# Differential attention: the combination of the two maps, shared by VectorE and GpSimd in single tiles of keys from five tiles on

## The reference

```python
def block(args):
    qi, st = args
    sc = jnp.einsum('bhmqd,bhmkd->bhmqk', qi, k).astype(jnp.float32) * scale
    mask = kpos[None, :] <= (st + jnp.arange(Q_BLOCK))[:, None]
    p = jax.nn.softmax(jnp.where(mask, sc, -jnp.inf), axis=-1)
    a = p[:, :, 0] - lam * p[:, :, 1]
    return jnp.einsum('bhqk,bhkd->bhqd', a.astype(v.dtype), v)
```

## Time and profile before

| | us |
|---|---|
| median of 3 runs | 2376.82 |
| the profiled execution | 2375.63 |
| its span, first to last instruction | 2373.8 |
| PE busy | 2285.4 |
| DVE busy | 1749.2 |
| ACT busy | 975.2 |
| POOL busy | 354.6 |

### The profile page before, as it was taken

The page is one execution under the profiler, slowest core; times in us unless marked ns, Lnnn a source line. Parts: engine busy times, 40 slices in busy tenths (PEclk is TensorE's granted clock), DMA queues, the critical chain, the costliest instruction groups (busy, mean ns, idle before and its releaser), DMA issues.

```text
span 2373.8 us, 31336 instructions
## 1 busy us (share of the span) xinstructions
PE 2285.4 (96%) x11618; PEld 1926.3 (81%) x11618; DVE 1749.2 (74%) x2660; ACT 975.2 (41%) x1598; POOL 354.6 (15%) x281
## 2 busy tenths in 40 slices
PE   5999999987999999999999999999999999999999
PEld 3987897766889888888888888888888888888887
DVE  5558796978989876877676767677687676767676
ACT  4532555458888854432322222233432322223231
POOL 0343043823355630000000000000000000000000
PEclk8999999988999999999999999999999999999999
DMA  7441434120000052111111111135101111111112
GB/s 261 156 155 46 151 116 151 49 98 27 15 14 23 10 163 77 54 54 36 62 44 55 51 53 53 53 123 195 63 28 44 62 44 53 53 53 53 53 53 88
DMA packets 108280, 177.68 MB, mean 75 GB/s; under 512 B 5512, under 2 KB 77468, under 8 KB 107164
## 3 DMA queue, kind: packets, MB, share of 16 engines
q1 hardware_dynamic: 108188, 176.45, 22.5%
HBM read 152.84 MB, written 23.59 MB: 74 GB/s over the span
## 4 chain that ended last, share of the span: by engine, by line
PE 83%; DVE 8%; DMA 3%; ACT 2%; issue 2%; POOL 1%; SPq 1%; ACTq 0%; DVEq 0%
PE ps L2486 10%; PE ps L2484 10%; PE ps L2485 10%; PE ps L2522 7%; PE ps L2521 7%; PE ps L2523 7%; PE ps L2187 6%; PE ps L2188 6%; PE ps L2189 6%; PE ps L2374 2%; PE ps L2431 2%; PE ps L2429 2%; PE ps L2430 2%; PE ps L2359 2%; DVE sb_scores L1816 2%
## 5 line engine op out<-in xcount | busy, mean ns | idle before, releaser
L1974 DVE TENSOR_TENSOR sb_x_new<-sb_x_new,ps 128x512 f32<-128x512 f32 x512 | 347.2, 684 | 107.6 <-PE ps L2486 102.0
L2484 PE MATMUL ps<-sb_w_hi,sb_u_hi 128*128 128x512 f32 x1024 | 398.3, 389 | 0.0
L2485 PE MATMUL ps<-sb_w_lo,sb_u_hi 128*128 128x512 f32 x1024 | 398.3, 389 | 0.0
L2486 PE MATMUL ps<-sb_w_hi,sb_u_lo 128*128 128x512 f32 x1024 | 398.3, 389 | 0.0
L2486 PEld LDWEIGHTS ps<-sb_w_hi,sb_u_lo 128*128 128x128 f32 x1024 | 192.3, 188 | 39.9
L2484 PEld LDWEIGHTS ps<-sb_w_hi,sb_u_hi 128*128 128x128 f32 x1024 | 192.3, 188 | 39.9
L2485 PEld LDWEIGHTS ps<-sb_w_lo,sb_u_hi 128*128 128x128 f32 x1024 | 192.3, 188 | 39.8
L2189 PE MATMUL ps<-sb_h_hi,sb_w_lo 128*128 128x512 f32 x512 | 199.4, 389 | 0.0
L1418 ACT ACTIVATE ps<-ps 128x512 f32<-128x512 f32 x28 | 16.3, 582 | 410.8 <-PE ps L2523 410.8
L2187 PE MATMUL ps<-sb_h_hi,sb_w_hi 128*128 128x512 f32 x448 | 178.0, 397 | 0.7 <-DVE sb_w_lo L1935 0.7
L2188 PE MATMUL ps<-sb_h_lo,sb_w_hi 128*128 128x512 f32 x448 | 174.4, 389 | 0.0
(11 more groups left out here) (286 smaller groups left out, 4955.4 us busy)
## 6 DMA issues: line engine op xcount, KB each, us to landing
sb_w_full<-in_w_ff SPq DMA_DIRECT2D x34, 1024.0 KB, 5.1
sb_w_full<-in_w_ff SPq DMA_DIRECT2D x56, 512.0 KB, 3.8
sb_w_raw<-in_w_in SPq DMA_DIRECT2D x16, 1024.0 KB, 5.7
sb_ada<-in_w_ada SPq DMA_DIRECT2D x32, 512.0 KB, 5.3
sb_ada_first<-in_w_ada SPq DMA_DIRECT2D x8, 1024.0 KB, 14.3
sb_x_in<-in_x SPq DMA_DIRECT2D x16, 512.0 KB, 4.9
sb_mix_in<-mix_scratch SPq DMA_DIRECT2D x16, 512.0 KB, 5.1
sb_x_new<-in_x SPq DMA_DIRECT2D x16, 512.0 KB, 4.8
```

What stands on the lines that cost most here:

```text
L1974: V.tensor_tensor(out=y, in0=y, in1=psum[:, 4 + p % 4, :], op=ALU.add).then_inc(ff2_read, 1)
L2484: M(dst, uh, wh[:, j, col], start=j == order[0], stop=False, skip_group_check=fast)
L2485: M(dst, uh, wl[:, j, col], start=False, stop=False, skip_group_check=fast)
L2486: ins = M(dst, ul, wh[:, j, col], start=False, stop=j == order[1], skip_group_check=fast)
```

## The change

The split is now made in tiles and not in groups: from n = 5 on, DVE has the first half of the tiles, rounded up, and POOL the rest. DVE's part at n = 5 to 16 goes from 5, 6, 7, 4, 8, 8, 8, 8, 8, 8, 8, 8 tiles to 3, 3, 4, 4, 5, 5, 6, 6, 7, 7, 8, 8. POOL's goes from 0, 0, 0, 4, 1, 2, 3, 4, 5, 6, 7, 8 to 2, 3, 3, 4, 4, 5, 5, 6, 6, 7, 7, 8. PE waits for POOL at the group that holds POOL's first tile, which is group 0 at n = 5 and 6, group 1 at n = 7 to 14, and group 2 at n = 15 and 16. The counters of `upper_ready` now count the units with a POOL part from unit 16 on. n = 8, 15 and 16 keep their sizes.

```diff
 def upper(u):
-    n = len(at_groups(u))
-    return (n + 1) // 2 if u // HEADS + 1 >= 8 else n
+    n = u // HEADS + 1
+    return (n + 1) // 2 if n >= 5 else n
...
-UPPER_NO = running(int(upper(u) < len(at_groups(u))) for u in range(UNITS))
+UPPER_NO = running(int(upper(u) < u // HEADS + 1) for u in range(UNITS))
...
             def combine_upper(u):
-                n, c0 = (u // HEADS + 1) * P, upper(u) * BLK
+                n, c0 = (u // HEADS + 1) * P, upper(u) * P
                 if c0 < n:
                     pool.wait_ge(a_ready, u + 1)
...
-                both = upper(u) * BLK < n
+                both = upper(u) * P < n
                 if both and UPPER_NO[u] >= 4:
                     dve.wait_ge(upper_ready, UPPER_NO[u] - 3)
-                n = min(n, upper(u) * BLK)
+                n = upper(u) * P
...
                     if f == 0:
                         pe.wait_ge(a_ready, i + 1)
-                    if f == upper(i):
-                        pe.wait_ge(upper_ready, UPPER_NO[i] + 1)
+                    if f == upper(i) // 4 and UPPER_NO[i + 1] > UPPER_NO[i]:
+                        pe.wait_ge(upper_ready, UPPER_NO[i + 1])
```

## The result

The changed kernel takes 2392.43 us (median of five runs, 2391.16 to 2394.78), the kernel before 2379.27 in its five (2375.77 to 2383.40): the ratio is 1.0058, interval 1.0043 to 1.0072. It is slower, as forecast and inside the range, but by 13.2 us between the medians. The forecast's sum was +9.2 on one execution of 2375.63; the profiled execution of the changed kernel took 2394.78, which is +19.2. So the direction was right, and the sum was about half of what the two traces show.

What follows compares the result with a forecast made beforehand. In the attention at n = 5 to 14, PE, DVE and ACT, all nearly full, wait for each other. Terms -4.5 + 8.8 + 2.5 + 2.4 = +9.2 us on 2375.63 give 2384.8, as median 2386.0; range 2373 to 2393.

Steps and rivals of the forecast that it cites:

- term 4: PE's clock: one fall to half speed after the wait at n = 6, +2.4 us, bounds 0 and +8.
- a difference as a sign of being wrong: Behind the attention no slack was seen; a difference showing there would mean the forecast is wrong.
- part 2: POOL's long block of root and scalings delays PE at n = 6, 10 and 14: +4.0, +3.0, +1.8, sum +8.8 us.
- parts 1 and 3: Shorter DVE combinations at n = 5 to 14, -4.5 us; DVE held by POOL's instructions, +2.5 us.
- more falls of the clock: Rival: the clock falls at n = 10 and 14 too, +5 us on top, 2391; chance 0.13.
- Absorbed: Rival: PE makes up the block's delays and holds fall where DVE waits anyway, +0.4 us, 2377.2; chance 0.17.
- faster: Rival: three quarters of the shorter combinations' gain returns, the block costs only plain extra time, -5.5 us, 2371.3; chance 0.15.
- PE waits in every unit of n = 5 and 6: Rival: PE waits for POOL at group 0, +2.4 us to the forecast, 2388.4; chance within the forecast's 0.55.

Runs made afterwards that it cites:

- e4: Changed kernel with PE's waits for POOL at units 22, 38 and 54 filled by 50, 36 and 40 identity transposes: 2387.58 us, ratio 1.0028.
- e3: Changed kernel with the split by tiles at n = 5 to 8 only, by groups of four from n = 9 as before: 2388.68 us, ratio 1.0030.
- e12: Changed kernel with POOL's inverse root and scalings mostly left out, for timing only: 2368.44 us, ratio 0.9949.
- e13: Kernel before with POOL's inverse root and scalings mostly left out, for timing only: 2372.41 us, ratio 0.9963.
- e1: Changed kernel with POOL's block cut in three, the first scaling one step later and the second two steps later: 2392.15 us, ratio 1.0044.
- e9: Changed kernel with POOL's block in five pieces, PE's turns moved, and squares, sums and root one step later still: 2368.28 us, ratio 0.9946.
- e11: Changed kernel split by tiles from n = 8 only, block in five pieces, turns moved, squares, sums and root a step later: 2373.70 us, ratio 0.9964.
- e10: Kernel before with POOL's block in five pieces, PE's turns moved, squares, sums and root one step later: 2372.68 us, ratio 0.9962.
- e6: Changed kernel with POOL's block cut in five pieces and PE's turns of finished rows moved later: 2374.29 us, ratio 0.9969.
- e8: Changed kernel split by tiles from n = 8 only, with POOL's block in five pieces and PE's turns moved: 2375.92 us, ratio 0.9971.
- e7: Kernel before with POOL's block cut in five pieces and PE's turns moved later: 2376.21 us, ratio 0.9973.
- e2: Changed kernel with the split by tiles from n = 8 only, all tiles up to n = 7 left to DVE: 2385.45 us, ratio 1.0028.

## Why the prediction was right and wrong

**What failed** is the size of term 4, "I take one fall there". The size of one was right: the fall at n = 6 cost 2.4 by e4. But all three waits brought one, 7.4 us in the attention against 2.4, and 3.3 more came behind it, where I had counted nothing and had named a difference as a sign of being wrong. That is 8.3 of the 10.0 us that the sum lacks against the profiled execution; part 2 has 2.2 more, parts 1 and 3 take back 0.8, and 0.2 lie ahead of unit 16. The rival "more falls of the clock", to which I gave 0.13, is what happened. I set its chance by one pause of 2.49 us without a fall and took that for evidence on waits of 3 to 5 us; and e3 shows that even for 2.5 us it was one draw of two.

- Parts 1 and 3, -4.5 and +2.5: together -2.0. The full change shows -2.8 outside the blocks, e12 against e13 -1.3. The mechanism and the sum hold; one by one they were not separated. The holds are real (2.22 for 0.62 us), but they fell on L1836 and not where I had put most of them: L1834 was to take above 1 us behind each split at n = 5 to 7, and took 0.22 to 0.88. The row of n = 9, for which the prediction allowed 1 us or none, got none.
- Part 2, +8.8 (4.0, 3.0, 1.8): 11.0 by e4 (5.7, 2.8, 2.5). The wait at n = 6 was foretold as 6.6 and was 6.56; POOL's part of unit 22 was to end at 605.1 and ended at 604.1. Its price was set too low: 4.0 of 6.6 us, where 5.7 were paid. At n = 10 I expected POOL's part at 685.1, and it came at 690.8: the 6.0 us by which unit 38 was already late explain that, so this term was right (2.8 for 3.0). At n = 14 it was 2.5 for 1.8.
- Part 4, +2.4: 7.4 + 3.3. That the 3.3 are the clock's is read from the traces (below); no run changed that pause alone.
- *Absorbed* and *faster* are out: PE stood at all three places, and at most 1.0 us was made up behind them (12.6 to 11.6 from unit 42 to 48).
- *PE waits in every unit of n = 5 and 6*: the rows show 0.53 and 0.31 us in units 20 and 21, half a microsecond or less, without weight.
- Slips in the working: POOL has 12 more combinations, 24 instructions and not 24 pairs. At n = 6 ACT was busy for 12.28 of 16.36 us, so not every engine was "within 15% of full"; this was my evidence against *absorbed*. PE's idle 2.35 of 16.36 us is 14%, not a fifth. The score read at 623.55 us began with L946 and was over when L938 began, so it says something of L946 alone. The absorbed cases add up to 0.18 where 0.17 was given.

Between the medians only 13.2 of the 19.2 us are left. The kernel before was profiled at the low end of its runs, with a mean granted clock of 0.987. Over its 72 further executions beside the experiments those at 0.986 to 0.988 took 2375.2 to 2380.4 us and those at 0.982 to 0.984 took 2379.1 to 2385.5; the five of the changed kernel are all at 0.980 or 0.981. The median of three runs that the forecast started from was 2.5 us below the median of five.

## What to carry to other kernels

Before work of the critical path is put into a queue that was half idle, look for the longest uninterrupted block in that queue, not at its share: here 8.3 us of normalisation, which had cost the kernel before some 5.5 us in the attention (e13), cost 11 us more of waiting and 7 of clock. Every pause of PE that may drop the clock is to be priced as if it did, also if one trace shows it without. What a fall cost here depended on the place: 3.3 us (e3) or 1.6 (e4) at n = 14, 3.5 at n = 10 and 2.4 at n = 6 (e4), nothing at n = 9 (e4). Cut the block and move each of its users, since e1 moved one wait only to meet the next.

## What the runs showed of the hardware

The clock does not follow from a pause's length alone. Pauses of 2.49 and 2.51 us at the same place ended in 1.00 and 0.50 (before and e3). A pause of PE for a score read at n = 14 was 2.02 us in e9 and 2.04 in e11; the 4 us from it, first of e11, then of e9:

```profile
769.74:773.74 4.00, 4.00 (x22) 3.82 (x23) 3.93 (x8) 2.80 (x4) 1.59 (x1) 0.67 0.00 0
```
```profile
770.00:774.00 4.00, 4.00 (x33) 3.73 (x34) 3.93 (x8) 2.91 (x5) 1.68 (x1) 1.00 0.00 0
```

And the 2.01 us behind the attention, which every kernel has, left e9 at full speed and e10 at 0.50, here the stretches behind it, first of e9, then of e10:

```profile
844.61:850.00 5.39, 5.39 (x50) 5.39 (x51) 4.46 (x2) 3.07 (x6) 1.17 (x1) 1.00 0.86 286
```
```profile
852.00:858.00 6.00, 6.00 (x30) 6.00 (x30) 2.38 (x2) 4.95 (x4) 0.00 (x0) 0.50 0.00 0
```

At n = 9 it happened behind still less. A pause of 1.53 us for a score read in the changed kernel and one of 1.55 at the same place in e12, with the 6.02 us from each:

```profile
665.98 0.74 PE L2394 MATMUL ps<-sb_k_stack,sb_q_stack 128*128 128x512 f32 x2 [1.53 <-DVE sb_scores L1816]
```
```profile
665.98:672.00 6.02, 5.18 (x39) 4.64 (x39) 5.81 (x15) 4.64 (x8) 2.19 (x2) 1.00 0.01 3
```
```profile
656.46 0.73 PE L2394 MATMUL ps<-sb_k_stack,sb_q_stack 128*128 128x512 f32 x2 [1.55 <-DVE sb_scores L1816]
```
```profile
656.46:662.48 6.02, 6.02 (x29) 5.58 (x30) 5.51 (x15) 3.88 (x6) 2.22 (x2) 0.59 0.01 3
```

e4, e6 and e8 have the pause there too, 1.54 to 1.55 us, and the clock fell behind it (0.72, 0.58 and 0.58 over the 6.0 us); e9 has one of 1.62 a unit later, which left it at 1.00.

The length of the slow stretch behind the attention tells what is lost there. It was 17 us in the changed kernel, e1, e3, e7 and e8; behind unit 63 they took 2.8 to 3.5 us more than the kernel before with its 6 us. e9 and e11 have none and took 3.0 and 3.2 us less. e7 is the kernel before in another placing, so the long stretch is no mark of the new division.

The three waits of the changed kernel (4.55 us and more) and those of e2 (4.55 and 5.04) all ended in slow turns of 1.09 us. The Trainium skill ("TensorE: Matmul & The Clock Gate", "HAM oscillation — how this bites in real kernels") lays the fall to pauses that are long enough; the long ones agree, and the pairs show that between 1.5 and 2.5 us something else than the length decides. What, and why the slow stretch behind the attention lasted 6 us in one execution and 17 in another, stays open: no run varied it alone. Nor did one tell how much of e9's lead over e10 is the division's and how much this draw. At one mean granted clock, 0.988, four executions of e9 took 2366.8 to 2369.0 us and three of e10, on another chip, 2370.3 to 2371.2, so it need not be the draw alone.
